# Order of work at two stage boundaries, and four v buffers instead of two, in a one-core decoder step on Trainium2

## What is computed

```python
def peer(x, w_query, keys1, keys2, exp_u, exp_v):
        q = (xc @ w_query).reshape(PEER_CHUNK, PEER_HEADS, D_QUERY)
        s1 = einsum('chk,nk->chn', q[..., :HALF_Q], k1)
        s2 = einsum('chk,nk->chn', q[..., HALF_Q:], k2)
        v1, i1 = top_k(s1, 16)
        v2, i2 = top_k(s2, 16)
        ...
        eid = e1 * N_KEYS + e2
        gate = softmax(sc)
        act = gelu(einsum('chkd,cd->chk', exp_u[eid], xc))
        out = einsum('chk,chkd->cd', gate * act, exp_v[eid])
```

## Time and profile before

| | us |
|---|---|
| median of 3 runs | 2163.32 (2163.17 to 2169.2) |
| the profiled execution | 2165.74 |
| its span, first to last instruction | 2163.9 |
| TensorE busy | 2004.1 |
| VectorE busy | 1454.9 |
| ScalarE busy | 678.4 |
| GpSimd busy | 398.4 |

### The profile page before, as it was taken

The page is one execution under the profiler, slowest core; times in us unless marked ns, Lnnn a source line. Parts: engine busy times, 40 slices in busy tenths (PEclk is TensorE's granted clock), DMA queues, the critical chain, the costliest instruction groups (busy, mean ns, idle before and its releaser), DMA issues. The chain is left out here.

```text
span 2163.9 us, 27907 instructions
## 1 busy us (share of the span) xinstructions
PE 2004.1 (93%) x9593; PEld 1706.4 (79%) x9593; DVE 1454.9 (67%) x3120; ACT 678.4 (31%) x1032; POOL 398.4 (18%) x473
## 2 busy tenths in 40 slices
PE   7999699999999996998699999999999999998884
PEld 6885466784577663776599999999999999997783
DVE  1113863211299996999778787888888887876554
ACT  2221232201111111989333333333333333323222
POOL 0000000000023322000232443443333323310000
PEclk9999555759999998999899999999999999999997
DMA  8000500212222111454688887898988888864433
GB/s 324 18 15 20 199 0 1 103 44 93 101 69 78 59 46 62 154 205 175 251 287 282 290 300 259 299 314 275 322 289 298 293 283 292 289 202 129 122 111 112
DMA packets 195788, 382.10 MB, mean 177 GB/s; under 512 B 13167, under 2 KB 134957, under 8 KB 192269
## 3 DMA queue, kind: packets, MB, share of 16 engines
q1 hardware_dynamic: 157733, 243.52, 33.3%
q0 software_dynamic: 36864, 134.23, 17.5%
q10 hardware_dynamic: 1056, 2.62, 0.3%
HBM read 343.51 MB, written 35.34 MB: 175 GB/s over the span
## 5 line engine op out<-in xcount | busy, mean ns | idle before, releaser
L1204 PE MATMUL bank<-p_high,v_high 128*128 128x416 f32 x1024 | 363.2, 355 | 29.3 <-DVE v_low L1608 29.1
L1204 PE MATMUL bank<-p_high,v_low 128*128 128x416 f32 x1024 | 361.8, 353 | 0.0
L1204 PE MATMUL bank<-p_low,v_high 128*128 128x416 f32 x1024 | 358.4, 350 | 0.0
L1158 PE MATMUL bank<-h_high,u_high 128*128 128x416 f32 x768 | 273.1, 356 | 23.2 <-DVE u_low L1608 19.1
L1158 PE MATMUL bank<-h_high,u_low 128*128 128x416 f32 x768 | 273.6, 356 | 0.0
L1158 PE MATMUL bank<-h_low,u_high 128*128 128x416 f32 x768 | 270.9, 353 | 0.0
L1374 POOL DMA_INDIRECT rows<-in_u_rows,row_u x128 | 173.7, 1357 | 472.3 <-issue 246.1
L1204 PEld LDWEIGHTS bank<-p_high,v_high 128*128 128x128 f32 x1024 | 192.7, 188 | 42.2 <-DVE v_low L1608 40.8
L1608 DVE TENSOR_TENSOR v_low<-vv,v_high 128x1024 fp32r<-128x1024 f32 x128 | 156.8, 1225 | 101.8 <-ACT v_high L1301 93.9
L1307 ACT CAST p_high<-gel 128x416 fp32r<-128x416 f32 x128 | 69.1, 540 | 460.1 <-DVE gel L1636 457.5
L413 PE MATMUL proj<-w_in_sb,xT 128*128 128x256 f32 (+1 forms) x880 | 193.8, 382 | 14.2 <-DMA w_in_sb<-in_w_in 14.2
(11 more groups left out here) (203 smaller groups left out, 2932.1 us busy)
## 6 DMA issues: line engine op xcount, KB each, us to landing
vv<-in_v SPq DMA_DIRECT2D x128, 512.0 KB
u<-in_uT SPq DMA_DIRECT2D x96, 512.0 KB
gates_kept<-staged SPq DMA_DIRECT2D x13, 2048.0 KB, 7.5
gate<-gates_kept SPq DMA_DIRECT2D x30, 832.0 KB
early<-in_uT SPq DMA_DIRECT2D x32, 512.0 KB, 3.6
w_in_sb<-in_w_in SPq DMA_DIRECT2D x4, 2048.0 KB, 21.6
wq<-in_w_q SPq DMA_DIRECT2D x16, 512.0 KB, 3.5
ckT<-in_ckT SPq DMA_DIRECT2D x8, 768.0 KB, 5.8
```

What stands on the lines that cost most here:

```text
L1158: ins = pe.matmul(a_ps[par][:, 0:DT], x[:, par, k], y, start=(k == 0 and n == 0), stop=(k == KT - 1 and n == 2))
L1204: ins = pe.matmul(y_ps[m % 4][:, 0:DT], x[:, of % 2, c, at:at + P], y, start=(c == 0 and n == 0), stop=(c == CG - 1 and n == 2))
```

## The change

- ScalarE's exponential stands behind the sixth of the nine early gelus of the last head; the last three gelus and the casts `h_high` come after it.
- TensorE turns the two key tensors as soon as it has finished the early products, and only the third transpose waits for the gates (into another bank). VectorE makes the row numbers and the `count` table right behind the shifted scores, then copies the turned keys, and then sums and divides the gates.
- GpSimd zeroes `yT`, behind the output projection, and `dots` and `y0`, behind the last gate product; VectorE did all three.
- `split_h` and the split of the first u slice stand before the 48th batch (`SPLIT_AT` = 47), and ScalarE's rounding of that slice inside the gate stage, behind its eleventh block.
- In parts 6 and 7 a group's pieces 2 and 3 use the buffers of u (`u`, `u_high`, `u_low`), which are free by then, so that there are four. A buffer is loaded again when the same piece of the group before has been multiplied. Every engine walks a list in which `w` is one piece further ahead.

```diff
@@ group_steps
+    if wide:
+        heavy = [("w", x[1] + 1) if x[0] == "w" else x for x in heavy]
+        if not entered:
+            heavy.insert([x[0] for x in heavy].index("w"), ("w", 1))
@@ route
+        def wide(part):
+            return isinstance(part, int) and part >= PARTS - LEAD
+        def piece(part, gg, m):
+            if wide(part) and m >= 2:
+                view = lambda x: x[:, m % 2].rearrange("p k e -> p (k e)").rearrange("p (c n) -> p c n", c=CG)
+                return view(u), view(u_high), view(u_low)
+            return vv[:, m % 2], v_high[:, m % 2], v_low[:, m % 2]
+        def of_group(part, gg, m):
+            return (*before(part, gg), m) if m < VS else (part, gg, m - VS)
@@ block.sync
             def load_v(part, gg, m):
                 g = GROUPS * part + gg
-                wait(sp, v_done, KT // VS * (VS * g + m - 1))
+                if wide(part) and m >= 2:
+                    sp.wait_ge(a_done, NK)
+                    if g > WIDE:
+                        sp.wait_ge(v_done, KT // VS * (VS * (g - 1) + m + 1))
+                elif wide(part) and g > WIDE:
+                    sp.wait_ge(v_done, KT // VS * (VS * (g - 1) + m + 1))
+                else:
+                    wait(sp, v_done, KT // VS * (VS * g + m - 1))
@@ block.tensor
-            pe.wait_ge(gates, 2)
             pe.wait_ge(decoded, 4 * PH)
             pe.wait_ge(s_taken, TILES * PH)
             for n in range(3):
+                if n == 2:
+                    pe.wait_ge(gates, 2)
...
-            ins.then_inc(slot_turned, 1)
+                ins.then_inc(slot_turned, 1)
@@ block.scalar
-                for q in early_after(n):
+                for q in early_after(n)[:6]:
                     gelu(q)
-            for k in range(KT):
-                nc.scalar.copy(h_high[:, k], h2T[:, k, P:T]).then_inc(h_rounded, 1)
             act.wait_ge(shifted, 2)
             nc.scalar.activation(tops[:, 0:4], tops[:, 0:4], ACT.Exp)
             nc.scalar.activation(tops[0:NS, 4], tops[0:NS, 4], ACT.Exp).then_inc(gate_exp, 1)
+            for q in early_after(PH - 1)[6:]:
+                gelu(q)
+            for k in range(KT):
+                nc.scalar.copy(h_high[:, k], h2T[:, k, P:T]).then_inc(h_rounded, 1)
...
+                if b == IN_GATES:
+                    round_u(EARLY, 0)
@@ block.gpsimd
+            pool.wait_ge(outed, 2 * TILES)
+            nc.gpsimd.memset(yT[:, :, P:T], 0.0).then_inc(y_zero, 1)
...
+            pool.wait_ge(g_done, DT)
+            nc.gpsimd.memset(dots[:], 0.0).then_inc(y_zero, 1)
+            nc.gpsimd.memset(y0[:], 0.0).then_inc(y_zero, 1)
@@ block.vector
+            dve.wait_ge(slot_turned, 2)
+            take_slots(0, e1T)
+            take_slots(1, e2T)
+            dve.wait_ge(slot_taken, 2)
+            nc.vector.tensor_copy(e1b[:], e1T[:, P:T]).then_inc(keys_made, 1)
+            nc.vector.tensor_copy(e2b[:], e2T[:, P:T]).then_inc(keys_made, 1)
             dve.wait_ge(gate_exp, 1)
...
+            dve.wait_ge(slot_turned, 3)
+            take_slots(2, wT)
-            nc.vector.memset(yT[:, :, P:T], 0.0)
...
             for n in range(BATCHES):
+                if n == SPLIT_AT:
+                    dve.wait_ge(a_done, EARLY)
+                    split_h()
+                    split_u(EARLY, 0)
-            nc.vector.memset(dots[:], 0.0)
-            nc.vector.memset(y0[:], 0.0).then_inc(y0_zero, 1)
-            dve.wait_ge(a_done, EARLY)
-            split_h()
-            split_u(EARLY, 0)
             run_parts(dve, group)
+            for m in range(2, VS):
+                split_v(PARTS - 1, GROUPS - 1, m)
             for m in range(KT):
-                if m % (KT // VS) == 1 and m // (KT // VS) + 1 < VS:
-                    split_v(PARTS - 1, GROUPS - 1, m // (KT // VS) + 1)
                 add(PARTS - 1, GROUPS - 1, m)
```

More of the change, by code:

```diff
@@ L89, with group_steps @@
 assert NG * CG == NK and NB * GB == DT
-def group_steps(gg, weigh, ahead, fetch, last):
+def group_steps(gg, weigh, ahead, fetch, last, wide, entered):
     heavy = []
@@ L898, in route @@
         making = Region(nc, sb.at, GEL_AT)
+        count = making("count", [P, NK, TB], BF16)
+        e1b, e2b = (making(n, [P, DT], BF16) for n in ("e1b", "e2b"))
         hot = making("hot", [P, HOTS, TB, NK])
@@ L980, in steps, with piece_in @@
             return group_steps(gg, not (known and part == gg == 0), fetch > 0, fetch // GROUPS,
-                               known and part == PARTS - LEAD - 1 and gg == GROUPS - 1)
+                               known and part == PARTS - LEAD - 1 and gg == GROUPS - 1,
+                               not fetch, not fetch and GROUPS * part + gg > WIDE)
+        WIDE = GROUPS * (PARTS - LEAD)
+        def wide(part):
[5 more added lines that the diff above has]
+            return vv[:, m % 2], v_high[:, m % 2], v_low[:, m % 2]
+        def piece_in(part, gg, m):
+            g = GROUPS * part + gg
+            if not wide(part):
+                return v_in[m % 2], 16 * (VS // 2 * g + m // 2 + 1)
+            if m >= 2:
+                return u_in[m % 2], 8 * (NK - EARLY) + 16 * (g - WIDE + 1)
+            return v_in[m % 2], 16 * (VS // 2 * WIDE + g - WIDE + 1)
         def first_row(part):
@@ L1076, in group @@
                     if what == "w":
-                        load_v(*before(part, gg), *at) if at[0] < VS else load_v(part, gg, 0)
+                        load_v(*of_group(part, gg, *at))
             run_parts(sp, group)
-            for m in range(1, VS):
+            for m in range(2, VS):
                 load_v(PARTS - 1, GROUPS - 1, m)
@@ L1199, in weigh @@
                 wait(pe, y_added, q - 3)
+                _, top, rest = piece(part, gg, of)
                 for c in range(CG):
@@ L1202, in weigh @@
                     low = p_low[:, CG * (gg % 2) + c]
-                    for n, (x, y) in enumerate(((v_high, high), (v_high, low), (v_low, high))):
-                        ins = pe.matmul(y_ps[m % 4][:, 0:DT], x[:, of % 2, c, at:at + P], y,
+                    for n, (x, y) in enumerate(((top, high), (top, low), (rest, high))):
+                        ins = pe.matmul(y_ps[m % 4][:, 0:DT], x[:, c, at:at + P], y,
                                         start=(c == 0 and n == 0), stop=(c == CG - 1 and n == 2))
@@ L1299, in round_v @@
             def round_v(part, gg, m):
-                act.wait_ge(v_in[m % 2], 16 * (VS // 2 * (GROUPS * part + gg) + m // 2 + 1))
-                nc.scalar.copy(v_high[:, m % 2], vv[:, m % 2]).then_inc(v_rounded, 1)
+                loaded, value = piece_in(part, gg, m)
+                act.wait_ge(loaded, value)
+                x, high, _ = piece(part, gg, m)
+                nc.scalar.copy(high, x).then_inc(v_rounded, 1)
             def round_p(part, gg, c):
@@ L1317, in group @@
                     if what == "w":
-                        round_v(*before(part, gg), *at) if at[0] < VS else round_v(part, gg, 0)
+                        round_v(*of_group(part, gg, *at))
                     if what == "c" and not phase:
```

74 lines of the change are left out of this document (35 added, 39 removed).

## The result

The changed kernel takes 2134.2 us, the kernel before 2166.3 us, medians of four executions each; the ratio is 0.984, with a 95% interval of 0.980 to 0.987, which is 28 to 43 us. The forecast was 37.6 us of gain (0.983) and 2126.0 us, with a range of 2118 to 2139. Of the 8.2 us between 2126.0 and 2134.2, 3.0 lie in the start of the sum: it took 2163.3 for the kernel before, the median of three executions, and not 2166.3. The profiled execution of the changed kernel took 2134.30 us, 31.4 less than the one of before.

The account below looks back on a forecast made before the run. TensorE was taken as the engine to follow, held up by waits for VectorE's preparation, u_low and v_low. Boundaries -7.1 and last stretch -30.5 sum to -37.6: from 2163.3 to 2125.7, said as 2126.0 us; range 2118 to 2139.

Parts of the forecast that it names:

- First boundary: Between routing heads and gate stage: first gate batch starts 9.3 us sooner, at 852.7; bounds 7.5 and 10.5.
- the sixth place: Exponential behind the last head's sixth early gelu: TensorE waits 1.3 us before the last early product.
- No drain behind the table load: ScalarE at the exponential: the load back takes 1.28 us, with no 1.38 us drain before the seventh gelu.
- Zeroing: yT, about 2.9 us, and y0, 1.8 us, zeroed on GpSimd while it is idle or waiting: cost nothing.
- Second boundary: Gate stage's end to third full product: gates 5.4 us longer, chain behind them 3.2 shorter, +2.2; bounds 0 and +4.
- Last stretch: Four v buffers from group 24: 31 pieces at 4.5 us instead of 5.6, gain 30.5 us, between 22 and 33.
- the entry: Change from two to four v buffers at groups 23 and 24: costs 3.1 us, as 1.4 and 1.6 to 1.7 of waiting.
- rival 2: Last stretch: SyncE's in-order queue holds loads back, buffers don't work, only the boundaries gain: 2156 us; chance 0.04.
- VectorE as the next bound: Last stretch: VectorE's series is 17.3 us a group against TensorE's 18.0, so TensorE sets the pace.
- rival 1: Last stretch: VectorE or late landings set the pace, about 5.0 us a piece, 15.5 less gained: 2141 us; chance 0.09.
- rival 4: Last stretch: four loads in flight come slower, at 100 GB/s a group takes 29.5 us: 2212 us; chance 0.02.
- rival 3: Boundaries give all, 10.5 us (keys at full clock, gathers not delayed), and a free entry gives 33: 2120 us; chance 0.06.

Follow-up runs that it names:

- s2: The kernel before with only the first boundary's edits (exponential behind the sixth gelu, keys turned first, yT zeroed by GpSimd): 0.996 of the kernel before.
- s4: The changed kernel with the exponential behind the ninth early gelu, ahead of the casts of h: shifted scores to first gate batch 15.65 us instead of 17.23.
- s11: The changed kernel run again, nothing changed: 1256.3 us from the shifted scores to the last product with v, 1260.7 in its first profile.
- s3: The changed kernel with the splits of h and first u, and ScalarE's rounding of that u, back behind the gate stage: 0.982 of the kernel before.
- s1: The kernel before with only the four v buffers from group 24 on: 0.987 of the kernel before, 27 us.
- s8: The changed kernel with three needless VectorE fills per last-stretch group, behind the multiplication: last u product to last v product 176.3 us.
- s10: The changed kernel with three needless VectorE fills per last-stretch group, behind the adds: last u product to last v product 189.5 us.
- s7: The changed kernel with four v buffers from group 23 on, one group sooner: 0.982; last u product to last v product 170.0 us.
- s9: The changed kernel with exponential behind ninth gelu, splits behind gates, row numbers first, fewer GpSimd store waits, four buffers from group 23: 2116.1 us, 0.975 of the kernel before.
- s6: The changed kernel with GpSimd not waiting for the last gate store and row numbers made right behind the last gate batch: 0.984 of the kernel before.

## Why the prediction was right, point by point

**First boundary: right, with one size off.** Forecast 9.3 us, measured 9.75 (and 9.8 alone, s2). TensorE's wait was 1.29 us for 1.3, the ten transposes took 1.53 for 2.0, and VectorE's and TensorE's steps in series came as they stood in the rows of before. The transposes follow the early products without a break, and the granted clock over them is 1.00; I had taken a value halfway to that bound. The forecast named the price of the sixth place (1.3 us), but it never weighed the ninth place with the casts behind it, which s4 shows to be 1.6 us better.

**No drain behind the table load: right.** The load back at 836.46 ends at 837.74 and the gelu starts at 837.75. The drain of 1.38 us that the Trainium skill gives (ScalarE: Activation LUTs, What ACT_TABLE_LOAD costs) isn't there. Nor is it ahead of a load: the sixth gelu ends at 826.50, and the load starts at 826.51.

**Zeroing: right.** yT's took 2.88 us on GpSimd (2.9 forecast), at 566.64, and GpSimd stood idle for 22.7 us behind it. y0's took 1.81 us under its wait for the store.

**Second boundary: right in mechanism and sign, 1 us short.** Forecast +2.2: the gate stage longer by 5.4, the chain 3.2 shorter. Measured: 5.9 longer in the first profile (180.7 for 174.9), 4.7 to 5.8 in the others with the splits inside, and L to C 25.05 for 27.43, 2.4 shorter: +3.5. The same code in s11 gives +2.6, and against s2, which has the first boundary but not this one, it is +2.3; so most of the miss lies within what repeats. The multiplication at L + 4.92 (4.85 forecast), the first gather at L + 10.88 (10.7). The terms that were off in this execution are the gate stage, 5.9 for 5.4, and the last step: I let the time from the first gather to the third product stay at 13.5 us (1064.30 - 1050.82), and it was 14.2. The first row came 5.9 us behind the first gather, 4.9 before. Why isn't shown. The u load that now is issued at the same moment (1042.91) isn't enough for it: in s3 it comes 2 us behind the first gather, as in the kernel before, and the step takes 14.8. s3 splits the part in two: the splits inside the gates cost 4.4 us, and the zeroing on GpSimd gives back 2.1. The forecast had only their sum, +2.2, and so didn't show that the zeroing alone would gain.

**Last stretch: mechanism right, the entry under-sized.** Forecast 30.5, measured 27.7 here (206.9 to 179.2) and 30.9 in s1, which has shorter entry waits. That 30.9 is so near to the forecast doesn't confirm the 3.1 us: s1's waits are 1.5, 0.3, 1.7 and 1.3 us, and don't stand where I had put them. The pieces are 4.5 us apart as forecast; the difference is in the 3.1 us for the entry. TensorE waited 2.8 us at the last piece of group 23 and 2.4 at the second of group 24. From D to the latter it took 36.9 us where 33.6 stood, 3.3 lost and not 1.4; the 31 pieces from there took 142.3 where the forecast adds up to 141.2. Two things were missing in it.

The first is the load. I had the waits come from VectorE's splits ahead of its adds. The adds do stand behind a split, but the split itself waits for ScalarE, and ScalarE for a load: 3.35 us at the last piece of group 23, 7.83 at the second of group 24, whose load waits for all of group 23 (issued at 1946.71, cast from 1950.62, split from 1951.70). TensorE's wait of 2.4 us there has this chain behind it. I had named that load under rival 2 and given it no price, and had put the second wait, 1.6 us, one piece later; in s1, s3, s4, s8 and s10 there is one at that place too, of 1.3 us.

The second is the clock: behind each of the two waits TensorE ran some nine matmuls at half clock, (0.35 - 0.19) x 9 = 1.4 us each. The Trainium skill (TensorE: Matmul & The Clock Gate, Why this matters for your kernels) advises against idle gaps between bursts of matmuls beyond a length that it gives, since the clock falls behind them. The gaps here are shorter than its figure, and the clock fell behind two of three all the same; the rows decide.

s7, which loads into four buffers one group sooner, leaves one wait of 1.8 us and gives 9.2, which confirms that the entry is where the time went.

**VectorE as the next bound: sized too high.** I added its series up to 17.3 us a group. It is 16.7 (from one group's start to the next, 1953.83 to 1970.57, while it catches up), so the slack is 1.3 and not 0.7, and s8 shows that more fits into its waits. In the changed kernel TensorE has no wait at all between 1980 and 2080 us, so rival 1 is out, and had less for it than I gave.

**The total.** The boundaries gave 6.3 us at the third product (1064.30 to 1058.04) for 7.1 forecast, the stretch 27.7 for 30.5, and the middle took 3.0 back, which the forecast didn't have. That is 31.0 of the 31.4 us between the two profiled executions. s11 shows that the middle's share isn't the change's: A to E is 1256.3 there, 35.4 us less than before, which is what the ratio gives. Rivals 2 and 4 are out: past the entry TensorE waits for no piece, and the DMA engines moved 166 GB/s in the stretch (133 in the group of the earlier trace rows). Of the three things that rival 3 wanted, keys turned at full clock, gathers not delayed and a free entry, only the first came.

## What to carry to other kernels

When work is moved from behind a barrier to before it, ask which chain ends last behind the barrier: here it was a small copy, a store and a gather, under which the splits are free (s3), while inside the saturated stage they cost their full 5 us. A buffer scheme is worth what its producer chain exceeds the consumer's step by, and its first round, where old and new order meet, is to be costed wait by wait: which load each split waits for, and the half clock that a wait of about 2 us may leave behind. To find an engine's slack, add work at several places: work put into a wait says nothing about the series.

## What the runs showed that I had not expected

- The middle stretch, whose code no kernel changes, differs by up to 9 us between executions (854.5 to 863.7), 4.1 of it between two of the same kernel, and by 11 us in when they reach the first boundary (826.8 to 837.9), while the boundaries repeat within 1 us. A difference of 5 us between kernels is visible in such distances, and hardly in medians of four runs.
- The first gather of s9 took GpSimd 2.55 us, those of the changed kernel and of s6 1.15. In s9 VectorE's split of u (1021.53, 1.24 us) had begun just ahead of it; in the others VectorE stood still when it began. The trace of the changed kernel says more on this. Of its gathers 94 began while VectorE stood still, and each took 0.93 to 1.15 us; 56 began inside a dot product of `use_row`, which reads two operands from SBUF, and 51 of these took over 1.5 us, up to 1.98; the 6 that began inside an add into `yT`, which reads one operand from SBUF and one from PSUM, took 0.94. Both kinds, from GpSimd's timeline; the second began inside VectorE's dot product of 1272.58 to 1273.80:

```profile
1265.78 0.94 POOL L1427 DMA_INDIRECT rows<-in_u_rows,row_u  x1 [3.93 <-DVE dots L1733]
...
1272.96 1.64 POOL L1427 DMA_INDIRECT rows<-in_u_rows,row_u  x1 [6.25 <-DVE dots L1733]
```

  The Trainium skill (SBUF — State Buffer, Who interferes with whom) says that VectorE and GpSimd share a pair of ports, and that a VectorE instruction with two inputs in SBUF contends with a GpSimd instruction that reads SBUF; the counts agree. The same section infers that such an instruction doesn't hold up the writing of a gather's descriptors, and here the gathers do take longer. That holds for the splits of u and v too: 12 of the 27 gathers that began inside one took over 1.5 us. The rest of the 2.55 us, beyond the 1.98 seen elsewhere, stays open; the last store was going on at that time.
- Half clock came behind idle times of 2.4 and 2.8 us in the changed kernel, but not behind one of 2.31 us; in s6 not behind one of 2.54 us (at 1938.47), in s2 behind one of 1.84 us (at 2017.0). So the length of the idle time alone doesn't tell, and what does isn't shown. In the kernel before it came behind one of 2.05 us, at 2031.77. TensorE's timeline of the kernel before, there:

```profile
2031.77 0.46 PE L1204 MATMUL bank<-p_high,v_high 128*128 128x416 f32 x1 [2.05 <-DVE v_low L1608]
...
2034.15 0.55 PE L1204 MATMUL bank<-p_high,v_high 128*128 128x416 f32 x1
2034.50 0.55 PE L1204 MATMUL bank<-p_low,v_high 128*128 128x416 f32 x1
```
